# A hybrid decoder layer on one core: chunk work at two places inside each projection panel, early norms, and local values with V stationary

## The chip, the cores and the metric

One core of one Trainium2 chip runs the whole kernel in one launch. The metric is device time in microseconds (us) from start to end, the median of several executions. The engines are TensorE (PE in the profile), VectorE (DVE), ScalarE (ACT), GpSimd (POOL) and SyncE (SP), which here issues the loads. Each engine runs its own list of instructions in order; the lists meet only at semaphores.

## The reference, cut to what matters

One decoder layer serves 1024 prompt rows and 8 x 4 sample rows, model width 1024. The part that the diff touches is the first sub-layer for the prompt:

```
h = rmsnorm(x, g_mix_pre)
z, xbc, dt, q, k, v = split(h @ w_in)        # 512 | 1024 | 8 | 512 | 128 | 128 columns
xbc = silu(causal_conv4(xbc))                # x 512 | B 2x128 | C 2x128
# SSD, 8 heads of 64, state 128, in chunks of 128 rows
y = (C B^T * decay) (x dt)  +  C state * decay_in  +  x * d_skip
u = rmsnorm_by_group(y * silu(z)) * g_ssd_norm
# local attention, window 128: 8 query heads, 2 key/value heads of 64
p = softmax([k_prev k_this] scores with a sink per head);  att = p @ [v_prev v_this]
mix = concat(u, att) @ w_out
```

Besides it the keys and values of 256 memory rows are projected (`rmsnorm(mem) @ w_xk`, `@ w_xv`). Cross-attention and the feed-forward network follow and are not touched.

## The kernel before

`build_mixers` takes the 1056 rows (the 32 sample rows are at the end) in three groups of 384, 384 and 288 rows. For a group the input projection is 19 panels of 128 output columns: panel 0 for dt, then 18 (8 of xBC, 4 of z, 4 of q, 1 of k, 1 of v). Full precision is kept by splitting both operands into a high and a low half and adding three products, so a panel is 8 k-steps x 3 = 24 matmuls (`panel`, L914). After the three groups 16 panels of 256 columns give the memory's keys and values (`mem_panel`, L1052); they go in pairs.

The weights of a panel are loaded into one of three buffers (`raw`), ScalarE copies the high half (`split_hi`, L374) and VectorE subtracts for the low half (`split_lo`, L611), each into one of two buffers, so panel n+2 is split once panel n is done (`hi_ahead`, `lo_ahead`). ScalarE evacuates a panel's result (`evac`, L379).

While group g is projected, the three chunks of group g-1 are worked off, each in six steps (`slots`, k = 0 to 5), one after each panel. A chunk has these pieces:

- scores of four heads (L972), mask and maximum on VectorE (`scores`, L739), exponentials on ScalarE (`softmax`, L461), transposes of the probabilities (L1012, L1016), their copies (L479, L798), and the values (`values`, L1025): probabilities stationary, V moving in 64 columns, 16 records a set of four heads. `attended` (L805) divides by the softmax sum, and `att_transposed` (L1040) brings the result into `mixT`.
- transposes of the convolved x and B (L952, L955), C B^T (L960), the decay matrix from `rr` (L325 on GpSimd, L965), within-chunk product (L996), state product (L988), new state (L1004).
- gated norm: square (L472), power on GpSimd (L347), product (`un`, L791), transposes (L1033).
- for the next chunk: convolution (`conv0` L419 on ScalarE, three taps L680 and L683 on VectorE), tanh, `xc`.

In the steps before, each engine first splits for and evacuates after panel n, then does the pieces of step k; TensorE does its pieces after the whole panel. The two first repeats of `slots` per group are a hardware loop (`Fori`), the third is written out.

At the end of a group come its successor's rows: `norm` (square on ScalarE, power on GpSimd L315, product on VectorE L620), eight transposes a tile of 128 rows (L926), copy to the high half (L395) and subtraction for the low half (L628). The next group's first panel waits for all of them. The steps for dt (`dt_part`, `dt_transposed`, `dt_sums` L943) lie in the third chunk of each group.

## Time and profile before

| | |
|---|---|
| median of 3 runs | 1885.03 us (1882.07 to 1886.67) |
| profiled execution, its own time | 1883.89 us |
| its span, first to last instruction | 1882.2 us |
| mean granted TensorE clock | 0.944 |
| VectorE, ScalarE, GpSimd busy | 48%, 40%, 10% |
| DMA | 121 GB/s over the span |

The span is what the trace shows; the profiled execution's time is 1.7 us more. Busy time is summed by engine; matmuls are pipelined, so a busy TensorE need not be at its peak. The granted clock is a share of full speed.

### The profile page before, as it was taken

To read this page: it belongs to the slowest core of one execution; us is meant where nothing else is said; L and a number is where in the kernel's file an instruction comes from. 1 tells how busy PE (TensorE), PEld (TensorE's weight loads), DVE (VectorE), ACT (ScalarE), POOL (GpSimd) and SP (SyncE) were. 2 spreads that over 40 slices of the span, in tenths; PEclk is the share of its full clock that TensorE was granted. 3 is DMA by queue.
4 is the path that set the end of the run, shared out by engine and by line. 5 is a ranking of instruction groups with operands and counts; after the bars stand their busy time and mean duration, and the time that the engine had idled before them with its cause. 6 is when DMAs were issued, how large, how long until landed. Compare 5 with 4: busy or idle time off the path is not lost. (4 is left out here: it accounts for less than half of the span.)

```text
span 1882.2 us, 28616 instructions
## 1 busy us (share of the span) xinstructions
PE 1706.9 (91%) x10924; PEld 1626.8 (86%) x10924; DVE 904.6 (48%) x1185; ACT 756.0 (40%) x1367; POOL 189.7 (10%) x301
## 2 busy tenths in 40 slices
PE   7979979887857789999999999999999999999996
PEld 7978878776745689889987899999999999999996
DVE  3356676765634336553343554443354443355543
ACT  3445454564432335443333533333233333244432
POOL 1021121111110001222222100000000000000000
PEclk9989978898977799999999999999999999999998
DMA  6522322321232645444445444444335444346561
GB/s 175 139 68 82 67 74 84 67 72 52 68 125 79 178 141 151 127 124 133 137 133 170 133 125 126 130 144 123 102 113 160 129 144 123 102 137 198 168 174 63
DMA packets 394141, 227.74 MB, mean 121 GB/s; under 512 B 33971, under 2 KB 384287, under 8 KB 394034
## 3 DMA queue, kind: packets, MB, share of 16 engines
q1 hardware_dynamic: 389442, 209.73, 38.8%
q0 software_dynamic: 4608, 16.78, 2.6%
q8 instruction: 59, 0.97, 0.2%
q14 instruction: 32, 0.26, 0.0%
HBM read 217.42 MB, written 10.07 MB: 121 GB/s over the span
## 5 line engine op out<-in xcount | busy, mean ns | idle before, releaser
L2611 DVE TENSOR_TENSOR ffn_lo<-ffn_raw,ffn_hi 128x1024 fp32r<-128x1024 f32 (+1 forms) x178 | 237.3, 1333 | 361.0 <-ACT ffn_hi L2539 361.0
L2678 PE MATMUL f_bank<-next_hi,ffn_hi 128*128 128x384 f32 (+1 forms) x1056 | 343.2, 325 | 10.1 <-DVE ffn_lo L2611 8.5
L2678 PE MATMUL f_bank<-next_lo,ffn_hi 128*128 128x384 f32 (+1 forms) x1056 | 342.1, 324 | 0.0
L2678 PE MATMUL f_bank<-next_hi,ffn_lo 128*128 128x384 f32 (+1 forms) x1056 | 342.0, 324 | 0.0
L2539 ACT ACTIVATE ffn_hi<-ffn_raw 128x1024 fp32r<-128x1024 f32 (+1 forms) x178 | 203.4, 1143 | 232.0 <-PE f_bank L2678 232.0
L2678 PEld LDWEIGHTS f_bank<-next_hi,ffn_hi 128*128 128x128 f32 x1056 | 199.6, 189 | 11.3 <-issue 9.2
L2678 PEld LDWEIGHTS f_bank<-next_lo,ffn_hi 128*128 128x128 f32 x1056 | 199.8, 189 | 0.0
L2678 PEld LDWEIGHTS f_bank<-next_hi,ffn_lo 128*128 128x128 f32 x1056 | 199.6, 189 | 0.0
L2678 PE MATMUL f_bank<-f_ahi,ffn_hi 128*128 128x384 f32 (+1 forms) x528 | 171.0, 324 | 0.2 <-DVE ffn_lo L2611 0.2
L2678 PE MATMUL f_bank<-f_ahi,ffn_lo 128*128 128x384 f32 (+1 forms) x528 | 170.4, 323 | 0.0
L2678 PE MATMUL f_bank<-f_alo,ffn_hi 128*128 128x384 f32 (+1 forms) x528 | 170.4, 323 | 0.0
L914 PE MATMUL bank<-a_hhi,a_whi 128*128 128x384 f32 (+1 forms) x456 | 161.3, 354 | 3.4 <-DVE a_hlo L628 3.4
L611 DVE TENSOR_TENSOR a_wlo<-a_raw,a_whi 128x1024 fp32r<-128x1024 f32 x73 | 89.6, 1234 | 138.2 <-ACT a_whi L374 138.2
L914 PE MATMUL bank<-a_hlo,a_whi 128*128 128x384 f32 (+1 forms) x456 | 154.6, 339 | 0.0
L914 PE MATMUL bank<-a_hhi,a_wlo 128*128 128x384 f32 (+1 forms) x456 | 153.9, 337 | 0.0
L2141 DVE TENSOR_TENSOR b_wlo<-b_raw,b_whi 128x1024 fp32r<-128x1024 f32 x72 | 93.0, 1293 | 122.6 <-ACT b_whi L2033 122.5
L2274 PE MATMUL b_bank<-b_ophi,b_whi 128*128 128x288 f32 (+1 forms) x320 | 107.0, 334 | 15.2 <-DVE b_wlo L2141 7.9
L374 ACT ACTIVATE a_whi<-a_raw 128x1024 fp32r<-128x1024 f32 x73 | 76.1, 1052 | 86.9 <-PE bank L914 81.4
L914 PEld LDWEIGHTS bank<-a_hhi,a_whi 128*128 128x128 f32 x456 | 93.5, 205 | 8.8 <-issue 4.9
L2274 PE MATMUL b_bank<-b_ophi,b_wlo 128*128 128x288 f32 (+1 forms) x320 | 100.6, 315 | 0.0
L2274 PE MATMUL b_bank<-b_oplo,b_whi 128*128 128x288 f32 (+1 forms) x320 | 100.6, 314 | 0.0
L2678 PEld LDWEIGHTS f_bank<-f_ahi,ffn_hi 128*128 128x128 f32 x528 | 99.3, 188 | 0.5 <-DVE ffn_lo L2611 0.5
(440 smaller groups left out, 3150.4 us busy)
## 6 DMA issues: line engine op xcount, KB each, us to landing
ffn_raw<-w_gate SPq DMA_DIRECT2D x66, 512.0 KB, 3.8
ffn_raw<-w_up SPq DMA_DIRECT2D x66, 512.0 KB, 3.8
ffn_raw<-w_down SPq DMA_DIRECT2D x48, 704.0 KB, 4.6
a_raw<-w_in SPq DMA_DIRECT2D x114, 256.0 KB, 3.3
b_raw<-w_xq SPq DMA_DIRECT2D x24, 512.0 KB, 4.2
b_raw<-w_xo SPq DMA_DIRECT2D x24, 512.0 KB, 4.3
xm<-x_prompt SPq DMA_DIRECT2D x16, 512.0 KB, 5.2
ffn_raw<-cache_mem_k POOLq DMA_DIRECT2D x16, 512.0 KB, 5.3
```

What stands on the lines that cost most here:

```text
L374: act.activation(w_hi[:, s2], raw[:, s3], ACT.Copy).then_inc(S["hi_done"], 1)
L611: dve.tensor_tensor(w_lo[:, s2], raw[:, s3], w_hi[:, s2].bitcast(F32), ALU.subtract).then_inc(S["lo_done"], 1)
L914: mm_ = pe.matmul(bank[s2][:, 0:w], a[:, s2, k, :], b[:, k, 0:w], start=(k == 0 and m == 0), stop=(k == KT - 1 and m == 2))
L2141: dve.tensor_tensor(w_lo[:, n % 2], raw[:, n % NRAW], w_hi[:, n % 2].bitcast(F32), ALU.subtract).then_inc(S["lo_done"], 1)
L2274: ins = pe.matmul(bank[n % 2][:, 0:w], a[:, n % 2, k, :], b[sl][:, k, 0:w], start=(k == 0 and m == 0), stop=(k == KT - 1 and m == 2))
L2539: act.activation(w_hi[:, s % 2, 0:kt], raw[:, s, 0:kt], ACT.Copy).then_inc(hi_done, 1)
L2611: dve.tensor_tensor(w_lo[:, s % 2, 0:kt], raw[:, s, 0:kt], w_hi[:, s % 2, 0:kt].bitcast(F32), ALU.subtract)\
L2678: ins = pe.matmul(out, a[:, s % 2, k, :], b[:, k0 + k, 0:w], start=(first and k == 0 and m == 0), stop=(last and k == kt - 1 and m == 2))
```

## The change

All engines now follow one list, `mixer_walk`, which names for every panel the pieces that lie at its four quarters; each engine supplies a function for the pieces that it has a part in. Pieces of the quarters 0 and 1 are done before the panel's first matmul, those of 2 and 3 before its k-step 4.

```
+def mixer_walk(do):
+    def place(at, j):
+        return lambda q: [do[what](*args) for p in ((q, q + 1) if q in (0, 2) else ()) for what, *args in at.get((j, p), ())]
...
+        at = {
+            (0, 0): [("pv", c - 1, 1)], (0, 1): [("uT", c - 1)], (0, 2): [("kq", c)],
+            (1, 0): [("sc", c, 0)], (1, 2): [("xT", c)], (1, 3): [("cb", c)],
+            (2, 0): [("seg", c)], (2, 1): [("den", c, 0)], (2, 3): [("zT", c)],
+            (3, 0): [("sc", c, 1)], (3, 1): [("pT", c, 0)], (3, 3): [("yd", c)],
+            (4, 0): [("yo", c)], (4, 1): [("cs", c)], (4, 2): [("pv", c, 0)], (4, 3): [("den", c, 1)],
+            (5, 0): [("usq", c)], (5, 2): [("pT", c, 1)],
+        }
...
+        conv = {(0, 0): [("cv0", later, 0)], (0, 1): [("cv0", later, 4)], (0, 3): [("tap", later, 1)], (1, 3): [("tap", later, 2)],
+                (3, 2): [("tap", later, 3)], (5, 0): [("cvt", later)], (5, 1): [("xc", later)], (5, 3): [("gates", later)]}
...
+            if i == 1:
+                extra = {(2, 2): [("nsq", 3 * g + 3)], (4, 3): [("nsq", 3 * g + 4)]}
+            if i == 2:
+                extra = {(0, 3): [("dtT", g)], (1, 1): [("dt1", g)], (1, 3): [("dt2", g)], (2, 2): [("cum", g)]}
+                if nt == 3:
+                    extra[2, 2] = extra[2, 2] + [("nsq", 3 * g + 5)]
+                extra[5, 2] = [("hT", *halves(g + 1)[0])]
+                extra[5, 3] = [("hT", *halves(g + 1)[1])]
...
+        more = [("hT", *x) for x in halves(g + 1)[2:]]
+        if g:
+            c = 3 * (g - 1) + 2
+            more = [("pv", c, 1)] + more[:2] + [("uT", c)] + more[2:]
```

The names: `kq` queries and keys, `sc` scores and softmax, `xT` transposes of x, B and V, `cb` C B^T, `seg` decay matrix, `den` softmax sum, `zT` gates, `pT` transposed probabilities, `yd`, `yo`, `cs` the three products of the SSD, `pv` values, `usq` and `uT` the gated norm, `cv0`, `tap`, `cvt`, `xc` the convolution, `nsq` the norm of a tile of rows, `hT` half of its transposes.

On ScalarE and VectorE a panel's pieces now come before the split for panel n+2 and the evacuation (ScalarE's function first, then VectorE's):

```
+            def panel(n, inner):
+                g, k = n // NPA, n % NPA - 1
+                for q in range(4):
+                    inner(q)
+                hi_ahead(n)
+                if k >= 0:
+                    evac(n, g, k, n % 2)
...
+            def panel(n, inner):
+                for q in range(4):
+                    inner(q)
+                lo_ahead(n)
```

In the memory stage two chunks (6 and 7) are spread over eight panels each, so all 16 panels have pieces; the scores' piece is at the middle of the second panel of each chunk. Everything is written out, without hardware loops.

The norm multiplies a tile of rows in place, in the panels of the group before. Its transposes go by halves (k-steps 0 to 3 of all tiles first), the first two in the middle of the group's last panel; they use banks 5 and 6 instead of 2 and 3. The next group's first panel waits for the first halves, and at k-step 4 for the others.

At the start all three tiles are normed, transposed and copied before the first weights are split (`consts`).

Local values have V stationary: 4 products of 256 columns a set, each of two filling 64 of the output's partitions, transposed as `mixT` wants them, so `attended` and `att_transposed` go. The division by the softmax sum is made on the probabilities by GpSimd:

```
+            def den(c, r):
+                pool.wait_ge(S["ri_done"], ready(2 * c + r))
+                pool.wait_ge(S["p_done"], ready(8 * c + 4 * r + 3))
+                pool.tensor_tensor(sc[:], sc[:], bc(ri[:, 4 * r:4 * r + 4].rearrange("p (h u) -> p h u", u=1), [P, 4, 2 * P]), ALU.mult)\
+                    .then_inc(S["pn_done"], 1)
...
-                for h in range(4):
-                    for m in range(2):
-                        mm_ = pe.matmul(bank[7][:, 256 * r + HD * h:256 * r + HD * h + HD], pt[:, 2 * h + m, :],
-                                        vw[:, m, HD * (h % 2):HD * (h % 2) + HD], start=(m == 0), stop=(m == 1))
+                for m in range(2):
+                    for v in range(2):
+                        mm_ = pe.matmul(bank[7][HD * v:HD * v + HD, 256 * r:256 * r + 256], vw[:, m, HD * v:HD * v + HD],
+                                        probs[:, :, v, m, :], start=(m == 0), stop=(m == 1), skip_group_check=True)
```

The sum for the gated norm adds the within-chunk product first (`yd`), then the state product (`yo`). The copy of the band into the mask is made once instead of in each chunk.

## Rows read from the trace of the kernel before

**Rows 1.** Page, part 1: busy us, share of the span, instructions.
```profile
PE 1706.9 (91%) x10924; PEld 1626.8 (86%) x10924; DVE 904.6 (48%) x1185; ACT 756.0 (40%) x1367; POOL 189.7 (10%) x301
```

**Rows 2.** Windows: length, busy by engine, granted clock, DMA share, GB/s.
```profile
18.73:106.66 87.93, 84.63 (x465) 83.88 (x465) 30.18 (x35) 34.78 (x54) 3.73 (x4) 0.98 0.49 126
106.66:121.76 15.10, 5.64 (x26) 4.38 (x25) 12.31 (x14) 7.61 (x13) 6.93 (x6) 0.66 0.23 66
121.76:264.20 142.44, 132.22 (x782) 123.76 (x783) 89.28 (x172) 72.99 (x175) 18.13 (x18) 0.93 0.29 75
264.20:281.36 17.16, 8.99 (x53) 7.40 (x53) 14.58 (x18) 8.70 (x18) 8.33 (x11) 0.67 0.23 57
281.36:416.27 134.91, 119.91 (x782) 110.79 (x783) 88.94 (x170) 70.24 (x171) 18.39 (x17) 0.89 0.29 77
416.27:433.42 17.15, 7.98 (x47) 6.52 (x45) 14.04 (x17) 7.91 (x18) 6.96 (x8) 0.71 0.15 45
433.42:542.81 109.39, 88.45 (x614) 80.89 (x614) 54.93 (x105) 43.66 (x122) 11.86 (x12) 0.90 0.23 71
```

**Rows 3.** Waits of PE, 0 to 600 us: total, times, longest us.
```profile
PE bank L926 <- DVE a_hn L620: 16.9, 6, 8.0
PE bank L1052 <- DVE a_wlo L611: 13.4, 5, 4.3
...
PE bank L1040 <- DVE k_att L805: 10.0, 6, 2.5
PE bank L1033 <- DVE k_un L791: 9.6, 6, 2.5
PE bank L943 <- DVE d_adt L670: 7.8, 3, 3.3
```

**Rows 4.** Timeline of PE: start us, us, then the instruction.
```profile
149.32 0.34 PE L914 MATMUL bank<-a_hhi,a_wlo 128*128 128x384 f32 x1
149.49 1.02 PE L988 MATMUL bank<-k_state,k_xc 128*128 128x256 f32 x4
150.35 1.89 PE L1025 MATMUL bank<-k_vw,k_pt 128*128 128x64 f32 x16
152.06 0.42 PE L914 MATMUL bank<-a_hhi,a_whi 128*128 128x384 f32 x1
```

**Rows 5.** Timeline of PE at the second scores of chunk 0.
```profile
144.15 1.13 PE L972 MATMUL bank<-k_kv,k_qs 64*128 64x256 f32 x8
145.22 0.45 PE L914 MATMUL bank<-a_hhi,a_whi 128*128 128x384 f32 x1
```

**Rows 6.** Groups of ACT, 121.76 to 264.20: busy us, mean ns, idle before.
```profile
L374 ACT ACTIVATE a_whi<-a_raw 128x1024 fp32r<-128x1024 f32 x18 | 18.9, 1052 | 26.1 <-PE bank L914 26.1
L461 ACT ACTIVATE k_sc<-k_sc,k_nb 128x256 f32<-128x256 f32 x24 | 11.9, 498 | 13.1 <-DVE k_nb L743 13.1
L419 ACT ACTIVATE xm<-a_proj,c_convb,c_convw 128x128 f32 (+1 forms) x24 | 9.8, 479 | 0.0
```

**Rows 7.** Groups of DVE, the same stretch.
```profile
L611 DVE TENSOR_TENSOR a_wlo<-a_raw,a_whi 128x1024 fp32r<-128x1024 f32 x18 | 22.6, 1256 | 34.7 <-ACT a_whi L374 34.7
```

**Rows 8.** Timelines of POOL and DVE from 211 us; then source L791, all.
```profile
211.37 1.65 POOL L347 TENSOR_TENSOR k_rsu<-k_rsu,c_mhalf 128x2 f32<-128x2 f32 x1
212.99 2.08 POOL L325 TENSOR_TENSOR k_rr<-c_triu,d_adt 128x512 f32<-128x512 f32 x2
...
213.06 2.16 DVE L791 TENSOR_SCALAR k_un<-k_yt,k_rsu 128x256 f32<-128x256 f32 x2 [0.59 <-POOL k_rsu L347]
...
L791 DVE TENSOR_SCALAR k_un<-k_yt,k_rsu x16: 346/1117/1126, 166.2 to 520.8; 128x256 f32<-128x256 f32 x16
```

**Rows 9.** Groups for the rows of x, 0 to 620 us.
```profile
L628 DVE TENSOR_TENSOR a_hlo<-bank,a_hhi 128x512 fp32r<-128x512 f32 (+1 forms) x22 | 13.8, 651 | 6.8 <-ACT a_hhi L395 6.5
...
L395 ACT ACTIVATE a_hhi<-bank 128x512 fp32r<-128x512 f32 (+1 forms) x22 | 11.9, 563 | 9.9 <-PE bank L926 9.9
...
L620 DVE SCALAR_TENSOR_TENSOR a_hn<-xm,a_rs,a_gpre 128x1024 f32<-128x1024 f32 (+1 forms) x9 | 11.3, 1276 | 8.6 <-POOL a_rs L315 8.6
```

More of the change, by code:

```diff
@@ L210, in build_mixers @@
         ]
+        skip = lambda *a: None
+        every = "start hT consts panel memory pv uT kq sc xT cb seg den zT pT yd yo cs usq cv0 tap cvt xc gates nsq dtT dt1 dt2 cum".split()
+        place = lambda c: (c // 3, c % 3)
+        where_of = lambda c: max(c - 1, 0) // 3
         @block.sync
@@ L226, in load_x @@
                     return
+                if t >= 3:
+                    sp.wait_ge(S["hT_done"], ready(max(ht_index(t - 3, h) for h in range(2))))
                 r = group_rows(t)
@@ L316, in norm, with through, kq @@
                     .then_inc(S["rstd_done"], 1)
[L318 to L320 removed]
+            def through(n, inner):
+                for q in range(4):
+                    inner(q)
+            def kq(c):
+                g, i = place(c)
+                adt = adts[g % 2]
                 pool.wait_ge(S["seg_done"], ready(c - 1))
@@ L347, in chunk, with cv0, start @@
                 pool.tensor_tensor(rsu[:], rsu[:], mhalf[:, 0:2], ALU.pow).then_inc(S["ur_done"], 1)
-            for t in range(3):
-                norm(t)
-            for ph in range(4):
-                g = ph - 1
-                if g >= 0:
-                    if g < 2:
-                        pool.wait_ge(S["evac_done"], ready(NPA * g + 1 + T_XBC + 7))
-                        pool.wait_ge(consts_done, k)
-                        pool.tensor_copy(proj[:, (g + 1) % 2, 0:8, 0:3], proj[:, g % 2, 0:8, 384:387]).then_inc(S["halo_done"], 1)
-                    with pool.Fori(0, 2 if g < 2 else 1) as i:
-                        chunk(g, i)
-                if g >= 0:
-                    chunk(g, 2 if g < 2 else 1)
-                if ph < 3:
-                    for t in range(3 * ph + 3, 3 * ph + (6 if ph < 2 else 5)):
-                        norm(t)
+            def cv0(c, j0):
+                g, i = place(c)
+                if j0 == 0 and i == 0 and g:
+                    pool.wait_ge(S["evac_done"], ready(NPA * (g - 1) + 1 + T_XBC + 7))
+                    pool.wait_ge(consts_done, k)
+                    pool.tensor_copy(proj[:, g % 2, 0:8, 0:3], proj[:, (g - 1) % 2, 0:8, 384:387]).then_inc(S["halo_done"], 1)
+            def start():
+                for t in range(3):
+                    norm(t)
+            mixer_walk(dict(dict.fromkeys(every, skip), start=start, panel=through, memory=through, kq=kq, zT=zT, den=den, yo=yo, usq=usq,
+                            cv0=cv0, nsq=norm))
         @block.scalar
@@ L604, in _ @@
+            mixer_walk(dict(dict.fromkeys(every, skip), start=start, consts=consts, hT=hT, panel=panel, memory=memory, cv0=cv0, cvt=cvt,
+                            gates=gates, kq=kq, xT=xT, seg=seg, sc=sc_, usq=usq, pT=pT, uT=uT, pv=pv, nsq=norm,
+                            dtT=lambda g: dt_part(g, 0), dt1=lambda g: dt_part(g, 1), cum=lambda g: dt_part(g, 2)))
         @block.vector
@@ new lines, in consts @@
+            def consts():
+                split_lo(0, 0, 0)
+                split_lo(1, 1, 1)
+                dve.wait_ge(consts_in, 16 * len(loads))
+                dve.wait_ge(consts_done, 19)
+                dve.wait_ge(S["cols_done"], ready(6))
+            mixer_walk(dict(dict.fromkeys(every, skip), start=start, consts=consts, hT=hT, panel=panel, memory=memory, nsq=norm, tap=tap,
+                            gates=gates, kq=kq, xc=xc_, xT=xT, cb=cb, seg=seg, sc=sc_, den=den_, yd=yd_, yo=yo, cs=cs, usq=usq, pT=pT,
+                            dtT=lambda g: dt_part(g, 0), dt1=lambda g: dt_part(g, 1), dt2=lambda g: dt_part(g, 2)))
@@ L1017, in p_transposed, with yd_ @@
                 mm_.then_inc(S["pT_done"], 1)
-            def values(c, r):
+            def yd_(c):
+                pe.wait_ge(S["mm_done"], ready(2 * c + 1))
+                pe.wait_ge(S["mixa_done"], ready(2 * c - 1))
+                pe.wait_ge(S["decay_done"], ready(min((c + 1) // 3, 2)))
+                for h in range(HEADS):
+                    mm_ = pe.matmul(bank[7][:, HD * h:HD * h + HD], mm[:, h, :], xdt[:, HD * h:HD * h + HD], start=True, stop=True)
+                mm_.then_inc(S["ydiag_done"], 1)
```

707 lines of the change are left out of this document (277 added, 430 removed).

## The prediction

> **What bounds the kernel now.** I read the page first: TensorE is busy 91% of the span, no other engine reaches half of it [rows 1]. A share over the whole span says nothing of the stage that the diff touches, so I cut the first 543 us where that stage's own steps begin and end [rows 2]. The reader is to see three kinds of stretch. Plain panels (18.73 to 106.66, group 0): busy 84.63 of 87.93. Panels with chunk work between them (121.76 to 264.20 and 281.36 to 416.27, groups 1 and 2, then 433.42 to 542.81, memory): idle 10.2, 15.0 and 20.9 us, at granted clocks of 0.93, 0.89 and 0.90. And three stretches in which rows of x are normed and transposed (106.66, 264.20, 416.27; 49.4 us together): busy 22.6 of it, at 0.66 to 0.71 of the clock. Together TensorE idles 73 us from 106.66 to 542.81. The waits name the owners [rows 3]: the transposes of x wait for the norm, the memory panels for the low half of the weights, the chunk's last two transposes for VectorE, the sums over dt for `adt`. Outside this stage the diff changes nothing, so 1882.2 - 542.8 = 1339.4 us are taken as they are.
>
> A panel is 24 matmuls, 0.173 us apart at full clock [rows 4], so 4.16 us; at 288 columns I scale this to 3.12. VectorE is busy 89 of 142 us in group 1 and 89 of 135 in group 2 [rows 2]: not the bound, but it walks its list in order, as ScalarE does, and their order decides.
>
> **Removed and added work on TensorE.** Local values go from 16 matmul records of 64 columns (1.71 us a set, 150.35 to 152.06 [rows 4]) to 8 records of 256. The trace has no such shape. Lower bound: the scores, 8 records of 256 columns on alternate halves of the array, took 1.07 us (144.15 to 145.22 [rows 5]). Upper: `k_state` with the full array, 4 records in 0.86 us [rows 4], so 8 in 1.72. I take the nearer, 1.1: 16 sets save 10 us of work, 0 at the other end. The four transposes of `att` go, some 0.45 us by the same rows, 8 times: 3.6 us. Twice as many switches between panels and pieces cost about 0.1 us each (after a piece the first panel matmul takes 0.25 to 0.28 instead of 0.17 [rows 4, 5]): 8 chunks x 6 = 5 us more. These three are inside the walk below, not beside it. The Trainium skill (TensorEngine Tiling (Array Packing), Key Properties) says that changing the tiling mode drains TensorE, which speaks against halves of the array placed between full-array panels. The scores' two sides cost only 0.1 us more than those of other pieces here, so by the trace 16 such sets are under 2 us, and the sum would move by that.
>
> **Added on GpSimd.** The division by the softmax sum moves from `att` (VectorE, 16 operations of 0.41 us on results) to the probabilities: 16 multiplications of 128x1024 on GpSimd, between exponential and transpose. Two 128x512 of it took 2.08 us [rows 8], so 2.1 each, now in the chain `den` to `pT` to `pv`.
>
> **Walk through one chunk of group 1.** Time 0 is the start of its panel 0 on TensorE. After each panel ScalarE makes a high half (1.05) and evacuates (0.47), then does its pieces; VectorE follows with the low half (1.25) about 2.45 after the panel's end, then its pieces [rows 6, 7]. Small operations are rounded from the same two views, where not all their rows stand here.
> Panel 0 has `pv` and `uT` (1.5) and ends at 5.8. ScalarE from 1.5: `pv` 0.4, `uT` 1.15, eight `cv0` 3.3, `kq` 1.0, so 7.3. Scores wait for `kq` behind all `cv0`: **wait 1.5**.
> Panel 1 ends at 13.8; softmax on ScalarE (four of 0.5, plus `es`) pushes its high half to 15.3. The low half is ready at 17.6, needed at 20.2.
> Panel 2 ends at 20.2. VectorE has `den` at 20.05, GpSimd's product is ready at 22.1 to 22.4. Panel 3: `sc` ends at 21.3, `pT` **waits 1.1**.
> Panels 3 and 4 end at 29.2 and 36.4; `yd`, `yo`, `cs`, `pv` find their data.
> Panel 5 ends at 41.5. `usq` on ScalarE 38.8, GpSimd's addition and power 1.9, so 40.7. GpSimd then starts `rr` of the next chunk at once, as it does now, and both `un` take 2.16 instead of 2 x 0.35 [rows 8]: 42.9. Then `xc` 1.2 and the copy of `pT` 0.7 stand ahead of what the next `pv` needs: 44.8. `pv` **waits 3.3**.
> Period 44.8. The chunks of group 1 take 46.9 to 49.9 us now with their last transposes, or (142.4 + 5.4 - 4.3)/3 = 47.8 with the first panel out (the last set of pieces, 5.4 us, lies behind 264.20). So about 3 us are won, partly lost again where dt, norm and transposes are added to the third chunk (tap 2 and dt2 come before `adt`: about 1 us wait in panel 2).
> Stretch 121.76 to 264.20: first panel 4.3, first chunk without `pv` 43.4, second 44.8, third 41.5, extras 5: 139, **-3**.
> Group 2, panels 1 us shorter, pieces the same: VectorE's and ScalarE's lists do not shrink. The same walk gives waits of 2.3 at the scores, 3.4 at `pT`, 4.2 at `pv`: period 43. With 3.2 for the first panel and 5 of extras, and 4 for a lower clock behind gaps above 3 us: 134.6, **0**.
>
> **The three norm stretches.** Norms are computed inside the group before; two of six half transposes (four in all for memory) are made in its last panel. What stays behind that panel: high half and evacuation 1.5, then two rounds of copy (0.56) and subtraction (0.65) per half [rows 9]. The next group starts on the first half of its rows: 5.0 us after group 0 (now 15.1), 7.4 after group 1 with `pv` and `uT` (now 17.2), 6.7 after group 2 (now 17.15): **-10, -10, -10**. What hides the eight norms is the third of the time in which VectorE idles in these groups [rows 2]; without it they cost 1.3 us each there [rows 9], 10 us.
>
> **Start.** All six copies now stand ahead of both splits of the first weights. Transposes end at 18.1, last low half of rows at 19.4, then high and low half of panel 0: 21.1 instead of 18.7: **+2.4**.
>
> **Group 0.** In the third part VectorE does tap 1 after eight `cv0` and dt before the low half: ready 10.2 for a panel due at 8.6, and `adt` 2.2 late. These 3.8 replace the 3.3 of now (part of the 7.8 of [rows 3]), and 0.9 of transposes come in: **0** within 1.
>
> **Memory.** Pairs of panels (5.8 us), both splits only after a pair, now behind the chunk's pieces. In each chunk's first pair the scores stand in the middle of the second panel, so softmax (2.2) stands ahead of the splits: TensorE waits 7 and 5 us there, 1.2 to 2.5 at the five other pairs. This gives 49 us for the first chunk, as now, and 45 for the second with its tail and 8 for a lower clock: 102 against 109.4, **-7**. The gain is that four panels no longer follow alone.
>
> **Sum.** 2.4 + 0 - 10 - 3 - 10 + 0 - 10 - 7 = -37.6. The profiled execution took 1883.9 us (span 1882.2 and 1.7 around it); 1846. The median of the runs shown is 1.1 above it: 1847; I round to **1847**. Semaphore steps I have not counted add about 5 at most; the bounds of `pv` move it by +5 or -2 where it lies on the path.
>
> **Rivals.** (a) *The chunks' waits go too.* Idle of 46 us in the three long stretches, 10 of which I already take, and 10 us for a clock of 1.0 there give 1847 - 36 - 10 = 1801. For: TensorE's own work is the least; VectorE has slack. Against: the walk finds three waits a chunk. (b) *GpSimd locks VectorE.* While `rr` ran, `un` took three times its time [rows 8]. 16 products of 2.08 us would take 33 us from VectorE; if all reaches the panels, 1880, no change to be measured. Against: two of them fall where VectorE waits for ScalarE. The Trainium skill (SBUF, Who interferes with whom) calls the shared ports an exclusive lock for two-input operations; the trace agrees for `un`, and this would make (b) as worked out here. (c) *Slower: weight halves come late.* They stand behind all pieces of a panel now instead of before them. In group 2 my walk has the low half at 17.6 for a panel due at 18.1. Each of 36 panels late by 1.5 us gives 54 us: 1901. It decides from 38/36 = 1.05 us a panel. For: memory pairs wait for it already, 13.4 us in five [rows 3]. Against: in groups 1 and 2 no panel waits for it now. (d) *Gaps only move*: what the norm stretches give back, the groups take (VectorE's 10 us of norms, later copies): 1884.
>
> **How the numbers follow.** Forecast 0.50 (1830 to 1866 of its own), (a) 0.15, (b) 0.14, (c) 0.13, (d) 0.08. A measurement here tells 0.3%, 5.7 us. (b) is half faster, half within. Faster 0.50 + 0.15 + 0.07 + 0.04 = 0.76, same 0.07 + 0.04 = 0.11, slower 0.13. The range reaches from near (a), 1806, to past (b) and (d), 1886, and leaves out (c) and the rest of (a).
>
> **What would show it.** Three gaps between groups of 5 to 8 us instead of 15 to 17; no wait for the norm; waits of `pT` for GpSimd's product, of scores for `kq`, of `pv` for `pT`'s copy; two waits of 5 to 7 us for the weights' low half in memory; first panel at 21. The prediction is wrong if the stretches of groups 1 and 2 change by over 10 us each, or if waits for the low half appear in them.

## The result: 50 us faster, where 38 were forecast

The changed kernel takes 1835.10 us (1833.27 to 1836.47, 4 runs); the kernel before, on the same chip, 1885.85 (1882.07 to 1886.83, 4 runs). The ratio is 0.9734, 95% interval 0.9717 to 0.9751. The forecast was 1847, in a range of 1806 to 1886: the sign and the range hold, the size falls 12 us short.

The page of the kernel after, part 1 (answers to [rows 1]):

```profile
PE 1675.8 (91%) x10764; PEld 1584.1 (86%) x10764; DVE 900.2 (49%) x1162; ACT 754.6 (41%) x1375; POOL 215.4 (12%) x317
```

TensorE has the same share of a shorter span. GpSimd has 25.7 us more: 32.2 for the products with the softmax's reciprocals, 6.5 less in all its other instructions. The stage must be cut into its stretches again (answers to [rows 2], same columns; the last row runs to the first transpose of the next block):

```profile
0.00:21.22 21.22, 6.08 (x25) 4.75 (x26) 9.10 (x11) 10.35 (x20) 7.06 (x29) 1.00 0.59 175
21.22:108.76 87.54, 84.70 (x473) 83.42 (x474) 39.64 (x43) 37.99 (x62) 5.20 (x8) 1.00 0.53 136
108.76:113.38 4.62, 2.57 (x18) 1.99 (x16) 3.08 (x5) 2.91 (x5) 0.00 (x0) 0.89 0.32 85
113.38:252.60 139.22, 128.21 (x748) 113.90 (x746) 96.79 (x174) 76.98 (x187) 37.14 (x34) 0.95 0.31 80
252.60:259.25 6.65, 4.81 (x29) 3.77 (x28) 5.35 (x8) 3.91 (x10) 0.00 (x0) 0.74 0.15 34
259.25:391.00 131.75, 109.84 (x747) 96.93 (x745) 94.16 (x171) 74.39 (x185) 36.99 (x32) 0.95 0.32 85
391.00:397.57 6.57, 2.89 (x22) 1.84 (x20) 6.57 (x10) 3.95 (x10) 0.50 (x1) 1.00 0.13 36
397.57:501.91 104.34, 84.96 (x574) 74.25 (x574) 54.40 (x100) 44.30 (x127) 20.27 (x16) 0.90 0.26 79
501.91:503.95 2.04, 0.00 (x0) 0.03 (x1) 0.00 (x0) 1.14 (x4) 0.52 (x4) 1.00 0.30 109
```

The memory's last panel ends at 499.78; 2.1 us of the eighth row are the last value products and transposes. Read against the forecast, in us:

| stretch | before | forecast | after |
|---|---|---|---|
| up to the first panel | 18.7 | 21.1 | 21.2 |
| group 0 | 87.9 | 88 | 87.5 |
| gap 1 | 15.1 | 5.0 | 4.6 |
| group 1 | 142.4 | 139 | 139.2 |
| gap 2 | 17.2 | 7.4 | 6.7 |
| group 2 | 134.9 | 134.6 | 131.8 |
| gap 3 | 17.2 | 6.7 | 6.6 |
| memory, to its last panel | 109.4 | 102 | 102.2 |
| the rest of the kernel | 1339.4 | 1339.4 | 1335.0 |

The three gaps give back 31.6 us, memory 7.2, groups 1 and 2 together 6.4. The waits of PE over 0 to 520 us tell what is left in the stage (total, times, longest; answers to [rows 3]):

```profile
PE bank L1027 <- issue: 17.9, 6, 4.6
PE bank L1051 <- DVE a_wlo L668: 16.4, 7, 4.6
PE bank L916 <- DVE xm L676: 11.9, 2, 8.1
PE bank L989 <- POOL k_sc L446: 7.2, 7, 2.8
PE bank L947 <- ACT k_qs L545: 5.4, 3, 2.3
...
PE bank L903 <- DVE a_wlo L668: 3.8, 2, 2.6
PE bank L937 <- DVE d_adt L724: 3.1, 2, 1.7
```

L1027 are the value products `pv`, put down to "issue" since the semaphore that came last isn't recorded; L1051 the memory's panels, L989 the transposes `pT`, L947 the scores, L937 the sums over dt. L916, the transposes of x, waits for a norm only twice, at the very start. Each kind of wait that the walk through a chunk names is there, but not in each chunk: the scores wait three times in six chunks, where the walk has six. A set of value products (timeline of PE: start, us; answers to [rows 4]):

```profile
149.38 1.08 PE L1027 MATMUL bank<-k_pt,k_vw 128*64 128x256 f32 x8
150.39 0.44 PE L903 MATMUL bank<-a_hhi,a_whi 128*128 128x384 f32 x1
```

From its first record to the next panel's matmul are 1.01 us; it was 1.71.

### The profile page after: what moved, and what is told of

It reads as the page before. It is cut to its first block and busy times, and to the rows that moved or that the text cites. A ratio compares the mean times of both kernels' runs of the same rounds, so it can differ in the third digit from the quotient of the medians.

```text
span 1834.8 us, 27884 instructions
## 1 busy us (share of the span) xinstructions
PE 1675.8 (91%) x10764; PEld 1584.1 (86%) x10764; DVE 900.2 (49%) x1162; ACT 754.6 (41%) x1375; POOL 215.4 (12%) x317
## 5 line engine op out<-in xcount | busy, mean ns | idle before, releaser
L903 PE MATMUL bank<-a_hlo,a_whi 128*128 128x384 f32 (+1 forms) x456 | 150.0, 329 | 0.0
L903 PE MATMUL bank<-a_hhi,a_wlo 128*128 128x384 f32 (+1 forms) x456 | 149.8, 328 | 0.0
L668 DVE TENSOR_TENSOR a_wlo<-a_raw,a_whi 128x1024 fp32r<-128x1024 f32 x73 | 98.3, 1356 | 80.5 <-ACT a_whi L484 80.4
L2210 PE MATMUL b_bank<-b_ophi,b_whi 128*128 128x288 f32 (+1 forms) x320 | 106.3, 332 | 11.9 <-DVE b_wlo L2077 7.8
L2614 PEld LDWEIGHTS f_bank<-f_alo,ffn_hi 128*128 128x128 f32 x528 | 99.4, 188 | 0.0
```

Source lines behind the costliest of these rows:

```text
L668: dve.tensor_tensor(w_lo[:, s2], raw[:, s3], w_hi[:, s2].bitcast(F32), ALU.subtract).then_inc(S["lo_done"], 1)
L903: mm_ = pe.matmul(bank[s2][:, 0:w], a[:, s2, k, :], b[:, k, 0:w], start=(k == 0 and m == 0), stop=(k == KT - 1 and m == 2))
L2210: ins = pe.matmul(bank[n % 2][:, 0:w], a[:, n % 2, k, :], b[sl][:, k, 0:w], start=(k == 0 and m == 0), stop=(k == KT - 1 and m == 2))
L2614: ins = pe.matmul(out, a[:, s % 2, k, :], b[:, k0 + k, 0:w], start=(first and k == 0 and m == 0), stop=(last and k == kt - 1 and m == 2))
```

## The experiments

Every kernel is the kernel after with the edit shown, and each was timed beside the kernel before, which took 1884.4 us in the runs of e1 to e4, 1883.5 in those of e5 to e8 and 1883.0 in those of e9 to e12. The table has the lengths of the profiled execution, in us, cut at the first and last panel matmul of each group, then the time at which the memory's last panel ends, the rest of the span, and the median of the runs with its range and its ratio to the kernel before.

| kernel | start | g0 | gap | g1 | gap | g2 | gap | mem. | end | rest | median (range), ratio [95%] |
|---|---|---|---|---|---|---|---|---|---|---|---|
| after | 21.2 | 87.5 | 4.6 | 139.2 | 6.7 | 131.8 | 6.6 | 102.2 | 499.8 | 1335.0 | 1835.1 (1833.3-1836.5), 0.9734 [0.9717, 0.9751] |
| e1 norms late | 21.4 | 86.2 | 14.6 | 131.2 | 15.9 | 129.9 | 14.5 | 99.4 | 513.1 | 1334.1 | 1850.8 (1848.5-1853.6), 0.9832 [0.9796, 0.9867] |
| e2 small product | 21.3 | 87.3 | 4.9 | 134.0 | 5.8 | 125.3 | 7.7 | 97.4 | 483.7 | 1336.8 | 1821.9 (1817.3-1824.8), 0.9670 [0.9633, 0.9708] |
| e3 order of pv | 21.2 | 87.1 | 4.3 | 137.8 | 5.9 | 130.7 | 6.6 | 101.8 | 495.3 | 1337.1 | 1834.4 (1833.3-1834.7), 0.9739 [0.9706, 0.9773] |
| e4 one place | 21.6 | 86.3 | 6.1 | 138.0 | 7.6 | 134.7 | 9.4 | 108.2 | 511.9 | 1335.2 | 1851.4 (1848.8-1855.1), 0.9837 [0.9802, 0.9873] |
| e5 kq first | 21.3 | 87.7 | 4.6 | 142.9 | 5.9 | 138.0 | 7.6 | 102.4 | 510.4 | 1334.7 | 1843.2 (1839.5-1846.8), 0.9783 [0.9758, 0.9807] |
| e6 memory scores | 21.3 | 87.5 | 4.7 | 139.1 | 5.9 | 132.5 | 6.6 | 93.2 | 490.9 | 1333.5 | 1826.4 (1823.9-1836.3), 0.9714 [0.9676, 0.9751] |
| e7 rr after un | 21.3 | 86.9 | 4.2 | 134.1 | 5.0 | 130.1 | 5.7 | 100.8 | 488.1 | 1334.4 | 1823.7 (1814.8-1826.2), 0.9673 [0.9638, 0.9708] |
| e8 all four | 21.2 | 87.8 | 4.2 | 138.6 | 5.2 | 135.4 | 5.9 | 98.2 | 496.5 | 1342.8 | 1841.1 (1839.8-1843.0), 0.9779 [0.9756, 0.9802] |
| e9 same half | 21.1 | 87.1 | 4.2 | 143.4 | 6.3 | 137.1 | 8.5 | 97.4 | 505.1 | 1331.8 | 1838.7, one run |
| e10 old products | 21.2 | 87.8 | 4.6 | 141.4 | 6.3 | 134.2 | 8.0 | 100.1 | 503.5 | 1331.1 | 1844.3 (1836.3-1847.6), 0.9802 [0.9778, 0.9825] |
| e11 e6 and e7 | 21.2 | 88.0 | 4.3 | 135.6 | 5.0 | 125.3 | 5.7 | 93.8 | 478.8 | 1335.9 | 1818.8 (1810.3-1823.6), 0.9658 [0.9619, 0.9697] |
| e12 e11 and start | 20.1 | 86.8 | 4.2 | 134.0 | 5.0 | 130.0 | 5.7 | 95.4 | 481.3 | 1330.2 | 1815.6 (1812.9-1818.0), 0.9647 [0.9622, 0.9672] |

How far one execution's lengths carry can be read from e3: its sets of value products last as long as before, it has the same median, and yet its stage ends 4.5 us sooner. So a difference of a few us between two rows of lengths is read as nothing, and the medians decide. The kernel before reads 1883.0 to 1885.9 in the four sets of runs, so a difference between a median here and that of the kernel after carries up to 3 us besides.

**e1_norm_late: the norms and all half transposes back between the groups.**

```diff
-                extra = {(2, 2): [("nsq", 3 * g + 3)], (4, 3): [("nsq", 3 * g + 4)]}
...
-                if nt == 3:
-                    extra[2, 2] = extra[2, 2] + [("nsq", 3 * g + 5)]
-                extra[5, 2] = [("hT", *halves(g + 1)[0])]
-                extra[5, 3] = [("hT", *halves(g + 1)[1])]
...
-        more = [("hT", *x) for x in halves(g + 1)[2:]]
+        norms = [("nsq", 3 * g + 3 + i) for i in range(nt)]
+        more = [("hT", *x) for x in halves(g + 1)]
```

> The changed kernel with one part undone: the norms of the next rows and all six (four) half transposes stand between the groups again; halves, in-place rows and the walk stay. Theory (the norm stretches were the gain because the norms moved under the panels): the stretches of 4.6, 6.7 and 6.6 us go back to 13 to 17 each, and the groups give back 1 to 3 us each since VectorE has less to do: 1835 + 27 - 5 = about 1857. Rival (the split into halves and the transposes in the last panel made the gain, norms would have been short anyway): under 1843.

Measured: 1850.8, 15.7 above the kernel after. The windows of gaps 1 to 3 and of groups 1 and 2:

```profile
107.56:122.14 14.58, 5.93 (x26) 4.49 (x25) 8.77 (x9) 7.63 (x13) 7.07 (x8) 0.65 0.24 67
122.14:253.37 131.23, 122.84 (x740) 110.84 (x738) 91.49 (x171) 73.23 (x179) 30.52 (x26) 0.99 0.32 81
253.37:269.25 15.88, 7.40 (x38) 5.40 (x37) 10.87 (x12) 8.96 (x18) 6.09 (x8) 0.67 0.35 110
269.25:399.19 129.94, 111.53 (x738) 98.82 (x737) 91.57 (x170) 71.42 (x178) 32.17 (x26) 0.92 0.29 74
399.19:413.72 14.53, 6.03 (x31) 4.44 (x29) 9.51 (x11) 7.87 (x16) 5.25 (x6) 0.77 0.23 67
```

The gaps are again nearly as long as before the change (45.0 us against 17.9; before 49.4), at the same low granted clock of 0.65 to 0.77. The edit takes back two things at once, the norms and the transposes in the group's last panel. The trace tells them apart: the three gaps are 27 us longer than in the kernel after, and in them the transposes wait 20.5 us for norms (waits of PE, 100 to 420 us):

```profile
PE bank L915 <- DVE xm L675: 15.1, 6, 4.9
...
PE bank L915 <- DVE a_hn L675: 5.4, 2, 3.7
```

But groups 1 and 2 are 8.0 and 1.9 us shorter and memory 2.8, so that the early norms and transposes, worth 27 us in the gaps, cost some 11 to 14 elsewhere. Only part of this is waiting: TensorE idles 2.6 and 3.5 us less in groups 1 and 2. In group 1 the other 5.4 us are its busy time, at a granted clock of 0.99 instead of 0.95, and memory, which has no norm in its panels, is shorter with nearly the same waits. How much of the busy time the norms account for isn't shown: in e3, with the norms in place, group 1 has 126.0 us of it at 0.98. The forecast had the early norms cost nothing while VectorE had slack; rival (d) is right that part of the gain moves, at less than half of its size.

**e2_small_den: GpSimd multiplies 8 of every 256 probabilities; most of the division is left out.**

```diff
-                pool.tensor_tensor(sc[:], sc[:], bc(ri[:, 4 * r:4 * r + 4].rearrange("p (h u) -> p h u", u=1), [P, 4, 2 * P]), ALU.mult)\
+                pool.tensor_tensor(sc[:, 0:4, 0:8], sc[:, 0:4, 0:8], bc(ri[:, 4 * r:4 * r + 4].rearrange("p (h u) -> p h u", u=1), [P, 4, 8]), ALU.mult)\
```

> The changed kernel, but GpSimd multiplies only 8 of each 256 columns by the inverse softmax sum, so 32 elements instead of 1024 per partition; most of the division is left out. Theory (the product costs only as a link between softmax and transposes): the 7.2 us of TensorE waits for it go, and what hung on them: 1835 - 10 = 1825, within 5. Rival (b) (it locks VectorE out of SBUF for 2.1 us sixteen times): 1835 - 25 to - 33, 1802 to 1810.

Measured: 1821.9, 13.2 less. One product falls from 1.89 us to 0.24 at the shortest (2.01 to 0.30 in the mean), and `pT` no longer waits for GpSimd. The groups of VectorE's low halves over 0 to 545 us, first after, then e2:

```profile
L668 DVE TENSOR_TENSOR a_wlo<-a_raw,a_whi 128x1024 fp32r<-128x1024 f32 x73 | 98.3, 1356 | 80.5 <-ACT a_whi L484 80.4
```

```profile
L668 DVE TENSOR_TENSOR a_wlo<-a_raw,a_whi 128x1024 fp32r<-128x1024 f32 x73 | 95.7, 1321 | 82.4 <-ACT a_whi L484 82.1
```

The mean falls by 35 ns, 2.6 us in 73 of them, not by the 33 us of rival (b). That isn't because the two engines leave each other alone. Where a product and a low half meet, the low half is held up; but most products run while VectorE waits for another engine. The trace of the kernel after, at two places:

```profile
294.14 1.89 POOL L446 TENSOR_TENSOR k_sc<-k_sc,k_ri 128x1024 f32<-128x1024 f32 x1 [4.17 <-DVE k_ri L813]
295.27 1.84 DVE L668 TENSOR_TENSOR a_wlo<-a_raw,a_whi 128x1024 fp32r<-128x1024 f32 x1 [1.22 <-ACT a_whi L484]
...
151.76 1.90 POOL L446 TENSOR_TENSOR k_sc<-k_sc,k_ri 128x1024 f32<-128x1024 f32 x1 [4.16 <-DVE k_ri L813]
153.94 1.23 DVE L668 TENSOR_TENSOR a_wlo<-a_raw,a_whi 128x1024 fp32r<-128x1024 f32 x1 [2.26 <-ACT a_whi L484]
```

Of the 16 products 12 overlap no instruction of VectorE. Of the 73 low halves 57 take some 1.22 us; the 16 that take 1.47 to 2.06 all overlap an instruction of GpSimd, two of them a product, and they are 9.8 us longer together (2 of 73, 1.0 us, in the kernel before). It goes both ways: a product that started while VectorE was at a low half took 2.85 us (at 369.06). So rival (b) falls by its size and not by its mechanism: the forecast had two products against it that fall where VectorE waits, and it is 12 of 16. What the product costs is its own time in the chain from scores to values, as the walk had it.

**e3_pv_order: the four products of a set go through one head's two halves of the keys before the other head's.**

```diff
-                for m in range(2):
-                    for v in range(2):
+                for v in range(2):
+                    for m in range(2):
```

> The changed kernel with the two loops of the local values exchanged: both products of one half of the array's columns, then both of the other, instead of alternating. Theory (the halves overlap only between neighbours that alternate): a set goes from 1.0 to about 1.7 us, 16 sets, 10 us in all, of which waits of the other engines hide about half: 1838 to 1845. Rival (they overlap in either order, or 1.0 us has nothing to do with halves): sets stay at 1.0 us, 1835 within 3.

Measured: 1834.4, no change, and the sets stay at 1.08 us. So the two heads need not alternate. This left open whether the two halves of the array overlap at all; e9 settles it.

**e4_one_place: TensorE does a panel's pieces of quarters 2 and 3 behind its last matmul, not inside** (quarter 1 goes with 0, so its call does nothing).

```diff
-                    if k in (2, 4, 6):
-                        inner(k // 2)
...
+                for q in (1, 2, 3):
+                    inner(q)
```

> The changed kernel, but TensorE does the pieces of the quarters 1 to 3 after the panel's last matmul instead of before k-step 4; order and all else unchanged. Theory (the second place matters, since it starts scores' followers half a panel, 1.6 to 2.1 us, earlier): each chunk longer by 2 to 3 us, memory too: 1835 + 20 = 1850 to 1860. Rival (only the order and the removed work matter, half a panel is hidden by the waits): 1835 within 5.

Measured: 1851.4, 16.3 more. The two longest groups of waits of PE, 0 to 520 us:

```profile
PE bank L1049 <- DVE a_wlo L668: 25.1, 7, 6.1
PE bank L1027 <- issue: 20.1, 6, 5.9
```

Not groups 1 and 2 pay, as I had expected, but memory (+6.0), the gaps (+5.2) and group 2 a little (+2.9): pieces that end later make the low halves and the values late, 8.7 and 2.2 us more in these two rows.

**e5_kq_first: ScalarE copies the queries and keys ahead of the convolution's first tap.** The expectation says ahead of the second; the edit puts them ahead of all eight `cv0`.

```diff
-            (0, 0): [("pv", c - 1, 1)], (0, 1): [("uT", c - 1)], (0, 2): [("kq", c)],
+            (0, 0): [("pv", c - 1, 1), ("kq", c)], (0, 1): [("uT", c - 1)],
```

> The scores wait for the query and key copies at the start of a chunk: three such waits in the changed kernel's trace, 5.4 us together (1.37, 2.29 and 1.69 us). This kernel lets ScalarE copy them ahead of the second convolution tap, one place earlier in the same panel. If the copy's place behind the tap is what makes the scores late, the three waits fall to under 1 us and the time to 1830 us (1828 to 1832), against 1835. Rival: the copy and the tap share one chain, so what was ahead now comes late; the next users of the tap's result wait instead, and the time stays within 1833 to 1838.

Measured: 1843.2, 8.1 more: the theory falls, and the rival's direction was right at more than its size. Waits of PE, 113 to 391 us, after and then e5:

```profile
PE bank L989 <- POOL k_sc L446: 7.2, 7, 2.8
PE bank L947 <- ACT k_qs L545: 5.4, 3, 2.3
```

```profile
PE bank L989 <- POOL k_sc L446: 13.9, 7, 3.7
PE bank L973 <- DVE k_mx L793: 4.7, 4, 2.4
```

The scores no longer wait, as meant. What waits is the next link: the tap that ScalarE now does second is what VectorE's taps build on, VectorE walks its list in order (its waits for the tap, L734 for L528, go from 11.6 to 14.0 us in group 1), and so the masked scores and the division come later: 11.4 us of new waits in this window for 5.4 removed. Two smaller waits fall too, so over the whole of groups 1 and 2 TensorE idles 36.9 us against 32.9. The two groups are 9.9 us longer; the other 5.9 are busy time at a granted clock of 0.93 in place of 0.95, which the waits alone don't explain.

**e6_mem_scores: in memory, the first scores move from the second panel to the third.**

```diff
-            (0, 1): [("kq", c)], (1, 2): [("sc", c, 0)], (2, 0): [("xT", c), ("cb", c)],
+            (0, 1): [("kq", c)], (2, 0): [("sc", c, 0), ("xT", c), ("cb", c)],
```

> In the memory's walk TensorE waits seven times for the weights' low parts (16.4 us in all), the two longest (4.62 and 4.16 us) right after VectorE's first masked scores, which its list puts ahead of the split of the next panel's weights. This kernel moves those scores from the second panel to the third, and nothing else. If VectorE's order is the cause, the two long waits fall under 1 us each and the stage from 102 to 94 us; time 1827 us (1825 to 1831). Rival: the masked scores are then late for the segment's product and the division, and as much is waited for there: 1833 to 1839.

Measured: 1826.4, 8.7 less; the stretch is 9.0 shorter. The windows of the memory's panels, after and then e6:

```profile
397.57:499.78 102.21, 83.14 (x562) 73.26 (x562) 54.40 (x100) 43.13 (x122) 20.27 (x16) 0.90 0.26 80
```

```profile
397.65:490.88 93.23, 79.36 (x562) 70.68 (x562) 55.42 (x100) 42.91 (x122) 21.24 (x16) 0.95 0.29 88
```

The two long waits for low halves fall from 4.6 and 4.2 us to 0.8 each, as expected, but two later ones grow (2.9 to 3.9, 1.2 to 2.0), so that the sum falls from 16.4 to 11.1. The other 3.8 are TensorE's own busy time for the same 562 records: its granted clock is 0.95 in place of 0.90. In the stretch with the wait of 4.6 us, 407.8 to 418.0, it is 0.67 in the kernel after; the like stretch of e6, 407.0 to 416.3, has 1.00. But e1 has the two long waits (4.3 and 4.2 us) and 80.6 us of busy time, so not all of the 3.8 can be put down to them. The median isn't clear of the kernel after by itself: one of the four runs took 1836.3, and the intervals overlap. That the stretch is shorter is seen twice, here and in e11 against e7 (93.8 and 100.8).

**e7_rr_after_un: GpSimd's decay matrix waits for VectorE's normalized values.**

```diff
                 pool.wait_ge(S["adt_done"], ready(g))
+                pool.wait_ge(S["un_done"], ready(2 * c - 1))
```

> GpSimd computes the decay matrix (rr) of a chunk while VectorE normalizes the values of the one before; VectorE's pair of instructions there takes 2.16 us beside it and 0.7 us alone. In this kernel GpSimd waits until VectorE has normalized them. If this sharing makes the value products late (17.9 us of waits in the longest such group, six of them), each is 1 to 1.5 us shorter and the time 1826 us (1824 to 1830). Rival: the value products wait for ScalarE's copy of the transposed scores, which is not moved, and a decay matrix that comes later makes the segment wait: 1834 to 1842.

Measured: 1823.7, 11.4 less. VectorE's normalized values (group over 108 to 500 us), after and then e7, and third PE's waits for the value products in e7 (0 to 520 us):

```profile
L842 DVE TENSOR_SCALAR k_un<-k_yt,k_rsu 128x256 f32<-128x256 f32 x16 | 14.2, 930 | 10.1 <-POOL k_rsu L460 10.1
```

```profile
L843 DVE TENSOR_SCALAR k_un<-k_yt,k_rsu 128x256 f32<-128x256 f32 x16 | 4.9, 350 | 10.8 <-POOL k_rsu L461 10.8
```

```profile
PE bank L1028 <- issue: 8.1, 5, 2.6
```

930 ns become 350, and the waits of the value products fall by 9.8 us. The Trainium skill (SBUF, Who interferes with whom) has the shared port pair as a lock that one of the two engines holds for a whole instruction, and the issue order as what decides who is held. The trace agrees: an instruction of 0.35 us takes up to 1.13 behind GpSimd's, and the order alone took that away. (`un` reads one tensor and a factor for each partition; so it bears out the lock, and the low halves of e2, with both inputs in SBUF, are the case of two inputs of which the prediction speaks.) GpSimd's instruction now runs beside four low halves instead, each of them 2.06 us long (the mean goes from 1389 to 1453 ns over 108 to 500 us), where VectorE has slack.

**e8_all4: e5, e6 and e7, and VectorE makes the convolution's result (`xc`) behind its copy of the transposed scores.** The expectation says ScalarE of that last move; both steps are VectorE's.

```diff
-                (3, 2): [("tap", later, 3)], (5, 0): [("cvt", later)], (5, 1): [("xc", later)], (5, 3): [("gates", later)]}
+                (3, 2): [("tap", later, 3)], (5, 0): [("cvt", later)], (5, 3): [("xc", later), ("gates", later)]}
```

> The three edits of this set together, and ScalarE's copy of the convolution's result moved behind its copy of the transposed scores. If the waits are separate links, their gains add: 5 for the queries' copy, 8 in the memory, 9 for the values, 2 for the last move, 24 in all less some overlap, 1815 us (1810 to 1820). Rival: most of them are slack in one chain (projection panel, conversion, scores, division, transposes, values), and only the memory's is left: 1826 to 1832.

Measured: 1841.1, 6.0 more; both theories miss. The stage ends only 3.3 us sooner than in the kernel after, since the waits of e5 come back larger (waits of PE, 0 to 500 us):

```profile
PE bank L974 <- DVE k_mx L794: 14.4, 6, 4.7
PE bank L990 <- POOL k_sc L447: 13.2, 8, 3.7
```

And the block behind it, whose code is the same, takes 99.1 us to the first record of cross-attention where it takes 91 to 94 in all the others. The windows of its middle, after and then e8:

```profile
536.70:555.10 18.40, 18.40 (x113) 12.13 (x112) 12.37 (x28) 4.18 (x7) 0.00 (x0) 1.00 0.53 154
```

```profile
536.10:556.00 19.90, 19.90 (x93) 12.98 (x92) 8.96 (x21) 3.58 (x6) 0.00 (x0) 0.72 0.46 131
```

The waits of TensorE in this block are the same (30.1 us in both), the granted clock isn't. Why it fell there in this kernel isn't settled.

**e9_pv_same_half: both heads of a set are written to the same 64 partitions.**

```diff
-                for m in range(2):
-                    for v in range(2):
-                        mm_ = pe.matmul(bank[7][HD * v:HD * v + HD, 256 * r:256 * r + 256], vw[:, m, HD * v:HD * v + HD],
+                for v in range(2):
+                    for m in range(2):
+                        mm_ = pe.matmul(bank[7][0:HD, 256 * r:256 * r + 256], vw[:, m, HD * v:HD * v + HD],
```

> The four products of one head pair are written to the same 64 of the 128 output partitions, so that the two halves of TensorE's array can't work side by side; the values of one head overwrite those of the other, so half of the attention's result is left out. If the halves overlapping make the set short (1.08 us for its 8 records), it takes 8 x 0.21, some 1.7 us here. Rival: a stationary matrix of 64 columns costs less by itself, and the set stays at 1.0 to 1.1 us.

The order is that of e3, so e3 is the kernel to compare with. One head overwrites the other, so half of the attention's result is left out. Measured, timeline of PE:

```profile
147.31 1.94 PE L1027 MATMUL bank<-k_pt,k_vw 128*64 128x256 f32 x8
149.18 0.44 PE L903 MATMUL bank<-a_hhi,a_whi 128*128 128x384 f32 x1
```

The same 8 records on one half of the array take 1.87 us to the next panel's matmul, on two halves 1.01, and 1.02 in e3. The halves do overlap, in either order of issue (e3). The Trainium skill (TensorEngine Tiling (Array Packing), Key Properties) says that different tiles can load and multiply in parallel; this case agrees at a factor of 1.85. The one run took 1838.7; a single run can't tell that from the kernel after.

**e10_p_stationary: the value products as before the change** (the result isn't turned as `mixT` wants it, so the attention's part of the output is in the wrong arrangement).

```diff
-                        mm_ = pe.matmul(bank[7][HD * v:HD * v + HD, 256 * r:256 * r + 256], vw[:, m, HD * v:HD * v + HD],
-                                        probs[:, :, v, m, :], start=(m == 0), stop=(m == 1), skip_group_check=True)
+                        mm_ = pe.matmul(bank[7][:, 256 * r + HD * h:256 * r + HD * h + HD], pt[:, 2 * h + m, :],
+                                        vw[:, m, HD * (h % 2):HD * (h % 2) + HD], start=(m == 0), stop=(m == 1))
```

> The value products alone are made as before the change: the transposed scores stationary, eight products of 64 columns in each of 16 sets; the result is copied on as it is, without the turn that the earlier kernel made of it, so the attention's part of the output is in the wrong arrangement. The set goes from 1.08 to 1.7 us (1.71 in the kernel before); 16 sets make 10 us. All of these products lie ahead of a panel's matmuls on TensorE, so 1845 us (1842 to 1848) against 1835. Rival: the stages are held by the chain through scores, division and decay, and a longer set only shortens the wait that follows it: 1834 to 1840.

Measured: 1844.3, 9.2 more, though the four runs spread from 1836.3 to 1847.6 and the profiled one is the fastest. The group of PE over 21 to 500 us, after and then e10:

```profile
L1027 PE MATMUL bank<-k_pt,k_vw 128*64 128x256 f32 x120 | 18.9, 441 | 18.7 <-issue 17.9 <-DVE k_pt L848 0.9
```

```profile
L1027 PE MATMUL bank<-k_vw,k_pt 128*128 128x64 f32 x240 | 33.3, 299 | 19.1 <-issue 18.2 <-DVE k_pt L848 0.9
```

The waits just ahead of the sets are the same. Those further on aren't: over groups 1, 2 and memory TensorE idles 48.8 us against 52.0, so a longer set does shorten some waits behind it, the part of the rival that holds. In this execution, the fastest of the four, the stage ends only 3.7 us later (groups 1 and 2 are 2.2 and 2.4 us longer, the gaps 1.0, memory 2.1 shorter), and the rest of the kernel is 3.9 shorter. So it is the medians alone that speak for 9.2 us, near the 10 that the forecast put on the products; what the stage itself loses in the median isn't shown.

The two kernels also show the price of the switch between whole-array panels and sets on halves, at the same place in the list. The set in e10 (timeline of PE; compare that of the kernel after above, which starts 0.27 us behind the last panel matmul at 149.11):

```profile
149.29 0.34 PE L903 MATMUL bank<-a_hhi,a_wlo 128*128 128x384 f32 x1
149.46 1.89 PE L1027 MATMUL bank<-k_vw,k_pt 128*128 128x64 f32 x16
151.16 0.42 PE L903 MATMUL bank<-a_hhi,a_whi 128*128 128x384 f32 x1
151.42 0.34 PE L903 MATMUL bank<-a_hlo,a_whi 128*128 128x384 f32 x1
```

Into the set 0.17 us here against 0.27 on halves, out of it 0.26 against 0.28 (the three sets at full clock): some 0.12 us a set.

**e11_mem_rr: e6 and e7 together, and e12_mem_rr_start: with the first weights' splits among the first transposes** (shown for ScalarE; VectorE's the same).

```diff
             def hT(t, h):
...
+                if m in (2, 4):
+                    split_hi(m // 2 - 1, m // 2 - 1, m // 2 - 1, 32)
                 act.wait_ge(S["hT_done"], ready(m))
...
             def consts():
-                split_hi(0, 0, 0, 32)
-                split_hi(1, 1, 1, 32)
```

> The two edits that paid, together: in the memory's walk the first masked scores move behind the split of the next weights, and GpSimd's decay matrix waits for the normalized values. Alone they gave 1826 and 1824 against 1835. They act in different waits (weights' low parts; value products), so the gains add: 1815 us (1812 to 1818). Rival: in the memory both draw on the same slack of VectorE, so the sum gives less there: 1820 to 1824.

> The two edits, and ScalarE and VectorE split the first two panels' weights between the first half transposes of the start, as in the kernel before, not behind all six. If that order made the first panel late (21.2 us after the start, 18.7 before), it starts at 18.8 and the time is 2.4 us under the kernel with the two edits alone, 1812.6 if that has 1815. Rival: the halves then come later by what the splits take, and the first panel stays at 20.5 to 21.2 us: 1814 to 1816.

Measured: 1818.8 and 1815.6. Both beat the kernel before and the kernel after; their intervals overlap, so that e12 is faster than e11 isn't shown by the medians. The two edits add nearly in full: 16.3 of 8.7 + 11.4 = 20.1. (The interval of e11 overlaps that of e7 alone; what e6 adds to e7 is read from memory's 7.0 us.) The start of e12 (timeline of PE):

```profile
20.14 0.66 PE L904 MATMUL bank<-a_hhi,a_whi 128*128 128x384 f32 x1 [1.37 <-DVE a_hlo L686]
```

The first panel waits for the last low half of the rows, no longer for the weights, and comes 1.1 us sooner, not 2.4. The trace shows what else has moved: VectorE's first low half of the rows starts at 13.23 us in e12, behind all three norms of the start, where the kernel before has it at 11.06, and the transposes that reuse its bank wait for it. That this is the missing 1.4 us wasn't tried.

## Why the prediction was right, and where its terms were off

**Gaps: right.** 4.6, 6.7 and 6.6 us against 5.0, 7.4 and 6.7 forecast; no transpose of x waits for a norm after the start, and e1 puts the gaps back by undoing this part alone, 20.5 of the 27 us as waits for norms. What the forecast priced at nothing, the norms and transposes under the panels, costs: with them gone, e1 has group 1 8.0 us shorter, most of the 11 to 14 in all, part of it by a higher granted clock.

**Group 1: right**, 139.2 against 139, in part by luck. The kinds of wait are those of the walk, and so is the size of one: over groups 1 and 2 the scores wait 1.37, 2.29 and 1.69 us (1.5 and 2.3 forecast), `pT` for the product up to 2.8 (1.1 and 3.4), `pv` 2.4 and 3.8 in group 1, 3.2 and 4.6 in group 2 (3.3 and 4.2). But the walk has the first two in every chunk. In group 1 it adds up to 14.4 us for the three kinds, and the trace has 8.9. So 5.5 us of waits that weren't there made up for busy time that it had too low; the walk of this group had no term for the granted clock, which was 0.95, and none for the work of the norms. That over half of the waits of `pv` is GpSimd's hold on `un`, which the walk had in it, is shown by e7; that the product's price is its length in the chain, by e2.

**Group 2: 3 us short**, 131.8 against 134.6. The walk has 25.5 us for the three kinds of wait, the trace 17.6. Against this stand 4 us for a lower clock behind gaps; the granted clock was 0.95, the same as in group 1. How the difference of 3 us divides isn't settled: it is within what e3 shows between two executions.

**Memory: right**, 102.2 against 102, with the two waits named (4.6 and 4.2 us; 7 and 5 forecast, so 3.2 too dear) and five of 1.2 to 2.9 (1.2 to 2.5 forecast). e6 shows the cause, the softmax ahead of the splits, and its price of 9 us in this stretch.

**Start: right**, 21.2 against 21.1. e12 gets back 1.1 of the 2.4, so the cause given, the order of splits and copies, is half of it.

**Group 0: right**, 87.5 against 88.

**Value products: right for the set, open for the kernel.** 1.01 us a set against 1.1. From the last panel matmul ahead of a set to the first behind it are 1.28 us at full clock, and 1.88 in e10; 0.59 saved 16 times is 9.5 us. e10's median loses 9.2, its profiled execution 3.7 in the stage. The prediction weighed the Trainium skill (TensorEngine Tiling (Array Packing), Key Properties), by which a change of the tiling mode drains TensorE: e10 gives the switch at 0.12 us a set, 1.9 us in all, which is the "under 2 us" of the prediction.

**The term that failed is the last, "1339.4 us are taken as they are".** The rest came out at 1335.0, 4.4 less. Cut at the first records of cross-attention and of the feed-forward part, the three pieces are 91.7, 442.4 and 805.3 us before, and 92.2, 436.2 and 806.6 after: it lies in cross-attention. In the twelve kernels of the experiments, whose code there is the same, that piece takes 432.8 to 440.2. So the profiled execution of the kernel before had a long one, and I had only that one. The windows of its first 100 us, before and then after:

```profile
634.53:734.53 100.00, 92.90 (x550) 91.46 (x550) 47.70 (x43) 42.24 (x63) 8.13 (x17) 0.95 0.64 182
```

```profile
592.03:692.03 100.00, 95.64 (x593) 94.56 (x594) 52.72 (x47) 46.90 (x71) 9.84 (x21) 0.97 0.68 192
```

TensorE waits 2.7 us less there and has a higher granted clock, so it gets 43 more matmuls done. Whether the change causes this (transfers that start at another moment) or the kernel before just has such a state more often wasn't tried. The sum of the forecast gives 1846.3 for the profiled execution. The 4.4 here and 5.4 in the stage (3.1 in group 2, 1.6 in the gaps, the rest 0.4 or less each) make it 1836.5, as measured; the median is 1.4 below that, and the forecast had added 0.7 for the median of before and the rounding: 11.9 in all.

**The rivals.** (a), that the chunks' waits go too, didn't happen, but e11 shows that 16 of its 36 us can be had by two moves. (b) is refuted by e2 as worked out, while its mechanism is there: e7 shows it for `un`, and the low halves that meet GpSimd's instructions show it at up to 2.06 us instead of 1.22. (c) didn't happen in groups 1 and 2: no wait for a low half appears there; in memory it is what e4 makes worse. (d) is a part, by e1: 11 to 14 us of the 27 in the gaps.

## What to carry to other kernels

Walk through one period of the loop on all in-order engines at once, and name each wait: here it gave seven of eight stretches within 0.7 us. Then count the waits too, and not only the total: in group 1 the walk had 5.5 us of waits that weren't there, and a busy time as much too short hid it. Before you pull work forward on an in-order engine, list what it passes: e5 removed 5.4 us of waits and made 11.4, while moving work back (e6, e7) to where its engine has slack gave 9 and 11. Before you give GpSimd work, look at which of VectorE's instructions it will meet: here most products met none, since VectorE had just made their input and was waiting for another engine. And take the parts of a kernel that a change doesn't touch from several executions, since a single one may be off by more than the term in dispute.

## What the runs showed of the hardware

- One product of 128x1024 on GpSimd took 1.89 us at the shortest, 2.01 in the mean of 16. The low halves on VectorE (both inputs in SBUF) took 1234 ns in the mean before, 1356 after and 1321 with the small product. Alone one took 1.22 us; the 16 of 73 in the kernel after that took 1.47 to 2.06 each overlapped an instruction of GpSimd, and a product that began behind a low half took 2.85. Where VectorE's `tensor_scalar` met GpSimd's decay matrix it took up to 1.13 us instead of 0.35.
- Two halves of TensorE's array took 1.01 us for what one half took 1.87, and 1.02 with two products of a head in a row. Between whole-array panels such a set cost some 0.12 us more to enter and leave than a set on the whole array (e10).
- The same 327 records of an unchanged block took 54.3 us of TensorE's time in one kernel and 61.1 for 328 in another, at a mean granted clock of 0.66 and 0.62, with the same waits.
